# A two-block transformer kernel: attention of a group placed among the projections of the next, heads in row and column pairs, memory keys and values made in the first block

## The chip, the cores and the metric

The kernel runs on one core of one Trainium2 chip. The metric is the device time in microseconds (us) of one execution. Engines are named as the profile names them: PE is TensorE (matrix products; PEld its weight loads), DVE is VectorE, ACT is ScalarE, POOL is GpSimd, SP issues most DMAs. All data is f32; "fp32r" is a one-pass f32 format of PE.

## The reference, cut to what matters

The program is two blocks in sequence. The first is a dilated-window attention over three groups of eight heads and a convolutional feed-forward; the second a layer with three attentions (differential, windowed, and over a memory of 256 tokens), gates, and sixteen experts. The sequence is 512 tokens of width 1024.

```python
# first block: three groups, windows 128/512/2048, dilations 1/4/16, 8 heads of 64
proj = (h @ w_in).reshape(B, S, 3, 3, 8, 64)            # per group: q, k, v
for g, (window, dilation) in enumerate(ATTN_GROUPS):
    q = rms_norm(proj[:, :, g, 0], q_gain[g]) * scale
    k = rms_norm(proj[:, :, g, 1], k_gain[g])
    o, lse = dilated_window_attention(q, k, proj[:, :, g, 2], window, dilation)
weights = softmax(stack(lses), axis=0)
x = x + sum(weights * outs) @ w_out
x = x + conv_ffn(rms_norm(x, ffn_norm), ...)
# second block
h, m = rmsnorm(x, attn_norm_g), rmsnorm(mem, mem_norm_g)
o_da = rmsnorm(diff_attention(...), subln_g) * 0.8      # 8 heads of 128
o_wa = window_attention(...)                            # 16 heads of 64
mk, mv = split(m @ w_mem_kv, 2)                         # mem is an input: no dependence on x
o_xa = memory_attention(xa_q, mk, mv)                   # 4 heads of 256
x = x + (g0 * (o_da @ w_da_o) + g1 * (o_wa @ w_wa_o) + g2 * (o_xa @ w_xa_o)) @ w_out
x = x + expert_choice_ffn(rmsnorm(x, ffn_norm_g), ...)
return rmsnorm(x, final_norm_g)
```

## The kernel before

Everything is written by hand for each engine, with semaphores; the order of the code of an engine is the order in which it runs. A dense product is made in three fp32r passes: the weights are split into a high and a low part (`w_hi`, `w_lo`), the activations too, and high x high, high x low and low x high are summed. SP loads weights in chunks of 1 MB into a ring of four slots. POOL splits each chunk in two **halves**: it writes the high part (L457), then the low part (L460); ACT writes the high part of the halves in `by_act` (L775) and POOL only the low one. There are two buffers, so half i may be split once PE has used half i-2. One half feeds 24 PE products of 512 columns.

**First block.** PE takes the three groups one after the other. For each it makes eight blocks of queries and keys in `to_features` (L1332 to L1334), each followed by the mean square of the block before (L1405, a product with `mean64`), and four halves of values in `to_tokens` (L1348 to L1350). ACT squares (L620) and takes the root (L626), DVE takes the reciprocal (L920) and scales (L932). Then the attention of the group runs in **units** of four blocks of 128 x 128: scores (L1426 in group 0, L1429 after it) of one head against keys that are padded with zeros to 128 rows (`k1_odd` for the odd heads), mask and row maximum on DVE (L943, L946), exponentials on ACT (L636), four transposes on PE (L1455), the copy of these on DVE (L954), and the product with the values (L1444, L1447), whose result ACT copies (L648). There are 16, 8 and 8 units. Within a unit each step waits for the one before, and PE has the scores, transposes and value products of neighbouring units to fill in, nothing else.

After the last group comes the **combination**: PE transposes the row statistics (L1461), DVE copies them (L965) and works out a coefficient for each head, group and token (L967 to L980, with ACT's L650), PE spreads each over 64 rows (L1468), DVE multiplies and adds (L987, L990), ACT and DVE split the sum (L654, L995, L998), and the output product follows in `out_proj`.

**Second block.** The windowed attention (scores L1588, transposes L1595, value products L1617) runs in 16 units plus a tail, with the projection of `xa_q` spread over the slots by the table `FILL2` (`proj_part`, L1530 to L1532). POOL makes a mask scale for each pair of heads and splits one half between (L509, `split(stage["f2"] + p + 1)`). Then comes the **memory stage**: the norm of the memory tokens, their transposes (L1376), eight blocks of keys (24 products of 256 columns each, L1380 and L1332 to L1334), with a mean square of one differential head after each block, and four blocks of values (L1348 to L1350); DVE scales the differential heads there (L1143, L1145). Then the **memory attention** (scores L1657, transposes L1677, values L1667), and the gates. The experts' 16 x 24 chunks of 1 MB end the program.

## Time and profile before

| | us |
|---|---|
| median of 3 runs (lowest, highest) | 2649.49 (2647.84, 2649.54) |
| the profiled execution | 2650.34 |
| its span, first to last instruction | 2648.6 |
| PE / DVE / ACT / POOL busy in it | 2362.2 / 929.0 / 502.4 / 1026.7 |
| granted TensorE clock, mean | 0.973 |

The table of stretches in the rows below gives the busy time of each engine in one stage. A busy PE is not PE at its peak, and a group's busy share does not say whether it lies on the path: for that, read which stage has nothing else to do on PE. Times in the rows count from the start of the span.

### The profile page before, as it was taken

To read this page: it belongs to the slowest core of one execution; us is meant where nothing else is said; L and a number is where in the kernel's file an instruction comes from. 1 tells how busy PE (TensorE), PEld (TensorE's weight loads), DVE (VectorE), ACT (ScalarE), POOL (GpSimd) and SP (SyncE) were. 2 spreads that over 40 slices of the span, in tenths; PEclk is the share of its full clock that TensorE was granted. 3 is DMA by queue.
4 is the path that set the end of the run, shared out by engine and by line. 5 is a ranking of instruction groups with operands and counts; after the bars stand their busy time and mean duration, and the time that the engine had idled before them with its cause. 6 is when DMAs were issued, how large, how long until landed. Compare 5 with 4: busy or idle time off the path is not lost.

```text
span 2648.6 us, 27075 instructions
## 1 busy us (share of the span) xinstructions
PE 2362.2 (89%) x11257; PEld 1558.1 (59%) x11257; DVE 929.0 (35%) x1313; ACT 502.4 (19%) x1076; POOL 1026.7 (39%) x499
## 2 busy tenths in 40 slices
PE   6999968999998998898899999799988888888886
PEld 4777837888787866576678888433323233332322
DVE  5654674555102047665622264211110101111012
ACT  2324232112002034476321010100000000000001
POOL 5444605888778754453548887100000000000000
PEclk9999979999999999998999999799999999999999
DMA  4111201233222321111312225699999999999996
GB/s 145 65 48 48 80 16 48 96 96 98 102 101 69 102 72 32 37 44 33 127 48 96 96 96 221 243 417 417 418 418 418 417 417 416 416 418 417 418 417 282
DMA packets 172341, 527.43 MB, mean 199 GB/s; under 512 B 9954, under 2 KB 92091, under 8 KB 139451
## 3 DMA queue, kind: packets, MB, share of 16 engines
q1 hardware_dynamic: 169008, 521.17, 50.7%
q10 hardware_dynamic: 3211, 4.51, 0.5%
q8 instruction: 90, 1.47, 0.3%
q14 instruction: 32, 0.26, 0.0%
HBM read 523.56 MB, written 2.10 MB: 198 GB/s over the span
## 4 chain that ended last, share of the span: by engine, by line
PE 73%; DMA 13%; DVE 9%; ACT 2%; issue 2%; ACTq 0%; POOL 0%; SPq 0%; DVEq 0%; POOLq 0%
DMA arena<-in_w_exp_up 9%; PE ps L1332 9%; PE ps L1334 9%; PE ps L1333 9%; PE ps L1834 8%; PE ps L1807 7%; PE ps L1495 5%; DMA ring<-in_w_exp_up 4%; PE ps L1348 3%; PE ps L1349 3%; PE ps L1350 3%; PE ps L1765 2%; PE ps L1789 1%; PE ps L1551 1%; PE ps L1530 1%
## 5 line engine op out<-in xcount | busy, mean ns | idle before, releaser
L457 POOL TENSOR_TENSOR w_hi<-ring,one 128x1024 fp32r<-128x1024 f32 x208 | 406.2, 1953 | 504.8 <-PE ps L1334 243.9
L460 POOL TENSOR_TENSOR w_lo<-ring,w_hi 128x1024 fp32r<-128x1024 f32 x222 | 542.7, 2445 | 57.3 <-ACT w_hi L775 41.1
L1332 PE MATMUL ps<-h_hi,w_hi 128*128 128x512 f32 x840 | 335.1, 399 | 2.6 <-ACT arena L648 1.8
L1334 PE MATMUL ps<-h_hi,w_lo 128*128 128x512 f32 x840 | 327.2, 389 | 0.0
L1333 PE MATMUL ps<-h_lo,w_hi 128*128 128x512 f32 x840 | 327.0, 389 | 0.0
L555 POOL TENSOR_TENSOR arena<-arena 128x512 f32<-128x512 f32 x8 | 8.4, 1049 | 810.8 <-PE ps L1777 794.0
L1807 PE MATMUL ps<-arena 128*64 128x512 f32 x944 | 213.0, 595 | 42.8 <-DMA arena<-in_w_exp_up 42.8
L1807 PE MATMUL ps<-ring,arena 128*64 128x512 f32 x944 | 213.1, 595 | 41.7 <-DMA ring<-in_w_exp_up 40.1
L1332 PEld LDWEIGHTS ps<-h_hi,w_hi 128*128 128x128 f32 x840 | 157.7, 188 | 42.7 <-issue 5.6
L1333 PEld LDWEIGHTS ps<-h_lo,w_hi 128*128 128x128 f32 x840 | 157.7, 188 | 35.8 <-issue 4.3
L1807 PEld LDWEIGHTS ps<-arena 128*64 128x64 f32 x944 | 71.5, 137 | 180.9 <-issue 180.6
L1334 PEld LDWEIGHTS ps<-h_hi,w_lo 128*128 128x128 f32 x840 | 157.7, 188 | 33.3
L1807 PEld LDWEIGHTS ps<-ring,arena 128*64 128x64 f32 x944 | 71.1, 137 | 179.0 <-issue 176.8
L1268 DVE TENSOR_TENSOR arena<-ps,arena 64x1024 f32<-64x1024 f32 x32 | 39.3, 1227 | 287.6 <-ACT arena L853 286.9
L853 ACT ACTIVATE arena<-ps 64x1024 f32<-64x1024 f32 x32 | 30.8, 1010 | 568.1 <-PE ps L1807 568.1
L1277 DVE TENSOR_TENSOR x<-ps,x 128x512 f32<-128x512 f32 x64 | 42.9, 689 | 260.9 <-PE ps L1789 260.4
L920 DVE RECIPROCAL arena<-arena 128x512 f32<-128x512 f32 x24 | 80.5, 3353 | 63.1 <-ACT arena L626 63.0
L1834 PE MATMUL ps<-arena 128*64 128x512 f32 x432 | 95.7, 593 | 5.5 <-DVE arena L1299 5.5
L1021 DVE SCALAR_TENSOR_TENSOR arena<-ps,vec,arena 128x511 f32<-128x511 f32 (+1 forms) x88 | 59.9, 743 | 114.2 <-ACT arena L665 114.2
L1834 PE MATMUL ps<-ring,arena 128*64 128x512 f32 x416 | 92.2, 593 | 5.5 <-DVE arena L1299 5.5
L1306 DVE COPY arena<-ps 64x512 f32<-64x512 f32 x16 | 11.1, 694 | 223.8 <-PE ps L1834 223.8
L863 ACT ACTIVATE arena<-ps 64x512 f32<-64x512 f32 x16 | 9.5, 591 | 349.3 <-PE ps L1834 349.3
(324 smaller groups left out, 3916.6 us busy)
## 6 DMA issues: line engine op xcount, KB each, us to landing
ring<-in_w_exp_gate SPq DMA_DIRECT2D x59, 1024.0 KB, 24.1
ring<-in_w_exp_up SPq DMA_DIRECT2D x59, 1024.0 KB, 25.4
arena<-in_w_exp_gate SPq DMA_DIRECT2D x59, 1024.0 KB, 23.8
arena<-in_w_exp_up SPq DMA_DIRECT2D x59, 1024.0 KB, 25.5
arena<-in_w_exp_down SPq DMA_DIRECT2D x54, 1024.0 KB, 20.1
ring<-in_w_exp_down SPq DMA_DIRECT2D x52, 1024.0 KB, 22.0
ring<-in_w_in SPq DMA_DIRECT2D x34, 1024.0 KB, 5.2
ring<-in_ffn_w_up SPq DMA_DIRECT2D x22, 1024.0 KB, 5.0
```

What stands on the lines that cost most here:

```text
L457: nc.gpsimd.tensor_tensor(hi, w, one[:].unsqueeze(2).to_broadcast(list(w.shape)), ALU.mult).then_inc(w_high, 1)
L460: nc.gpsimd.tensor_tensor(lo, w, hi.bitcast(f32), ALU.subtract).then_inc(w_split, 1)
L920: V.reciprocal(rr[:, n % 2, :], rt[:, n % 2, :]).then_inc(rr_done, 1)
L1332: mm(o, w[0][:, k, :], h[0][:, k, 0:ntok], start=(k == 0), stop=False)
L1333: mm(o, w[0][:, k, :], h[1][:, k, 0:ntok], start=False, stop=False)
L1334: last = mm(o, w[1][:, k, :], h[0][:, k, 0:ntok], start=False, stop=(k == KT - 1))
L1348: mm(o, hi, w[0][:, k - k0, :], start=(k == 0), stop=False)
L1349: mm(o, hi, w[1][:, k - k0, :], start=False, stop=False)
L1350: last = mm(o, lo, w[0][:, k - k0, :], start=False, stop=(k == nk - 1))
L1495: last = mm(ps[:, 2 * t + half, :], tile_of(a_, f, t), w_[:, 0, half * 512:half * 512 + 512], start=(f == 0 and a_ is act_hi and w_ is w[0 ...
L1807: last = mm(ps[64 * i:64 * i + 64, c, :], xeT[:, k, a * CAP:(a + 1) * CAP], w[:, c * 512:c * 512 + 512], start=(k == 0), stop=(k == KT - 1))
L1834: last = mm(ps[64 * half:64 * half + 64, 4, :], act_e[:, f, :], w[:, j * D + half * 512:j * D + half * 512 + 512], start=(f == 0), stop=(f ...
```

## The change

1. **Order of work in the first block.** A group's values are now made first, then its queries and keys. The projections of group g+1 are cut into 24 pieces of 12 products (`v_part`, `qk_part`). Four of them, or six pieces of memory keys for the last group, run before the attention of group g, the others in its slots (`fills`, `FILL`). In the slots of the last group stand the memory's keys (`mk_part`), in the combination the memory's values (`mv_part`). `qk` and `v1` are doubled.
2. **Pairs.** A unit is now two heads over one or two query tiles. The scores of the two heads use rows 0 to 63 and 64 to 127 of PE, with no zero padding; in group 0 one product spans 256 keys. The value products of the two heads write rows 0 to 63 and 64 to 127 of one bank.
3. **Who does what.** ACT, not DVE, copies the transposes. DVE copies the raw block out of its bank (`raw`) and scales it later (`scaled`). Square, root and exponential now alternate on ACT. The projections use banks 4 to 7, the attention 0 to 3.
4. **Memory.** Its norm runs among group 0's projections. Keys and values go to DRAM during the feed-forward and come back before the windowed attention. ACT writes the high part of six halves, not of fourteen.
5. **Combination.** Four banks in turn; the row copies no longer wait for each other; the output product starts after all multiplications are done and two of the four parts are split.
6. **Second block.** The memory stage is gone. The mean squares of the differential heads are summed in one bank in slots 12 to 15 of the windowed attention (`da_sum`), whose projection of `xa_q` now takes 12 slots of 3, 3 and 2 steps in turn, not 16 of 4. One root and one reciprocal of 8 x 512 follow; eight products spread the result over the rows during the memory attention, where DVE scales the eight heads. Scores of the memory attention use two banks, not four.

```diff
-NORM_TILES = [TT, TT, TT, MEM // P, TT]
+NORM_TILES = [TT, MEM // P, TT, TT, TT]
...
-        for j in range(8):
-            FILL2[2 * j] = ((j, range(2)), (j, range(2, 4)))
-            FILL2[2 * j + 1] = ((j, range(4, 6)), (j, range(6, 8)))
+        third = (range(3), range(3, 6), range(6, 8))
+        for u in range(12):
+            FILL2[u] = tuple((i // 3, third[i % 3]) for i in (2 * u, 2 * u + 1))
...
+            split_rows(tok_chunks(w1, b + 2 * GW, GW), v_ps, TT * (g + 1))
             split_cols(col_chunks(w1, b, 2 * GW), qk_ps, 8 * g)
-            split_rows(tok_chunks(w1, b + 2 * GW, GW), v_ps, TT * (g + 1))
+        split_cols(col_chunks(wm, 0, D), mk_ps, 0)
+        stage["mem_v"] = len(halves)
+        for half in range(2):
+            split_rows(tok_chunks(wm, D + 512 * half, 512), mk_ps, 8 + 2 * (half + 1))
+        by_act = range(stage["mem_v"] + 2, len(halves))
...
+            for p in range(HEADS1 // 2):
+                units += [(g, p, [t]) for t in range(TT)] if g == 0 else [(g, p, [0, 1]), (g, p, [2, 3])]
...
+        def fills(g):
+            if g + 1 < GROUPS:
+                todo = [("v", 2 * m + i, part) for m in range(2) for part in range(2) for i in range(2)]
+                todo += [("qk", 8 * (g + 1) + b, half) for b in range(8) for half in range(2)]
+            else:
+                todo = [("mk", j, half) for j in range(8) for half in range(2)]
+            first, n = (4, 4, 6)[g], UB[g + 1] - UB[g] + 2
+            rest = todo[first:]
+            return [todo[:first]] + [rest[u * len(rest) // n:(u + 1) * len(rest) // n] for u in range(n)]
...
-                split(stage["f2"] + p + 1)
+                split(stage["f2"] + min(p + 2, 8))
...
+                for i in range(L + 4):
...
+                    for n in ended(g, i, "qk"):
+                        square(n)
...
+                    for n in ended(g, i - 1, "qk"):
+                        root(n)
...
+                        act.wait_ge(nm_done, u + 1)
...
+                    if 1 <= i <= L:
+                        act.wait_ge(t_ps, m + 1)
                         if m >= 2:
...
+                            act.wait_ge(pv_done, m - 1)
+                        A(pt1[:, m % 2, :], ps[:, 2, :], F.Copy).then_inc(pt_done, 1)
...
+            def scaled(n):
...
+                dve.wait_ge(rt_done, n + 1)
+                V.reciprocal(rt[:, n % 4, :], rt[:, n % 4, :]).then_inc(rr_done, 1)
+                dve.wait_ge(rr_done, n + 1)
+                dve.wait_ge(qr_done, n + 1)
+                V.scalar_tensor_tensor(out=o, in0=o, scalar=vec[:, gain:gain + 1], in1=r, op0=ALU.mult,
+                                       op1=ALU.mult).then_inc(qk_done, 1)
...
+                for i, f in enumerate(FILL[g][0]):
+                    fill(g, f)
+                    if i == 1:
+                        for n in [7] if g == 0 else ended(g - 1, UB[g] - UB[g - 1] + 2, "qk"):
+                            mean_sq(n)
...
+                    for f in todo[0:1]:
+                        fill(g, f)
+                    m = u - 1
+                    if 1 <= i <= L:
+                        pe.wait_ge(p_done, m + 1)
+                        if m:
+                            pe.wait_ge(pt_done, m)
+                        for j in range(4):
+                            last = nc.tensor.transpose(ps[:, 2, j * P:(j + 1) * P], sm[:, m % 3, j * P:(j + 1) * P], ident[:])
+                        last.then_inc(t_ps, 1)
+                    for f in todo[1:2]:
+                        fill(g, f)
+                    for n in ended(g, i, "qk"):
+                        mean_sq(n)
...
+            mv_part(1, 0)
+            mv_part(1, 1)
             pe.wait_ge(coef_done, 1)
...
+            def last_oT(i):
+                pe.wait_ge(oT_low, 4)
+                pe.wait_ge(mk_ev, 12)
+            pe.wait_ge(oT_low, 2)
+            pe.wait_ge(bc_done, 12)
             out_proj((oT_hi, oT_lo), 4, wo_ps)
...
+                def da_sum(h):
+                    pe.wait_ge(pjA, PJ[:J_M].count("A"))
+                    pe.wait_ge(on_sq, h + 1)
+                    mm(ps[0:DA_H, 3, :], head_col[:, 7 - h:15 - h], osq[:, h % 2, :], start=(h == 0), stop=(h == 7)).then_inc(on_ps, 1)
+                if 12 <= u < 16:
+                    da_sum(2 * (u - 12))
...
+            dve.wait_ge(on_rt, 1)
+            V.reciprocal(ort, ort).then_inc(on_rr, 1)
...
+                        mm(ps[:, 6 + h % 2, :], ident[0:DA_H, h:h + 1].to_broadcast([DA_H, P]), ort, start=True, stop=True).then_inc(on_ps, 1)
```

**PE in the attention of group 0.** Before, one unit after the other; `ps` is PSUM, `arena` the working memory, `ident` the identity:

```order
L1455 MATMUL ps<-ident,arena 128x128 [waits pt_done,p_done]
L1455 MATMUL ps<-ident,arena 128x128 x3
L1426 MATMUL ps<-arena 128x128 [waits sm_done]
L1426 MATMUL ps<-arena 128x128 x3
L1444 MATMUL ps<-arena 64x128 [waits pt_done]
L1444 MATMUL ps<-arena 64x128 x3
```

And after, one slot of group 0, in which half a block of group 1's queries stands (12 products, of which the first three and the last are shown):

```order
L1612 MATMUL ps<-arena 128x256 [waits sm_done]
L1612 MATMUL ps<-arena 128x256
L1490 MATMUL ps<-h_hi,w_hi 128x512 [waits w_split,qr_done,sq_done]
L1491 MATMUL ps<-h_lo,w_hi 128x512
L1492 MATMUL ps<-h_hi,w_lo 128x512
...
L1492 MATMUL ps<-h_hi,w_lo 128x512
L1623 MATMUL ps<-ident,arena 128x128 [waits pt_done,p_done]
L1623 MATMUL ps<-ident,arena 128x128 x3
L1504 MATMUL ps<-arena,mean 128x512 [waits sq_done,rt_done]
L1640 MATMUL ps<-arena 64x128 [waits pt_done]
L1640 MATMUL ps<-arena 64x128 x3
```

The scores are two products of 256 columns where four of 128 stood, and a piece of the projection and now and then a mean square stand between a unit's steps.

**ACT in the attention of group 0.** Before, two units (L636 the exponentials, L648 the copy of a head's result):

```order
L636 ACTIVATE arena,l<-arena,nm 128x256 [waits nm_done]
L636 ACTIVATE arena,l<-arena,nm 128x256
L636 ACTIVATE arena,l<-arena,nm 128x256 [waits nm_done]
L636 ACTIVATE arena,l<-arena,nm 128x256
L648 ACTIVATE arena<-ps 64x512 [waits pv_done]
```

And after, two slots (L652 square, L659 root, L700 exponentials, L708 the copy of the transposes):

```order
L652 ACTIVATE arena<-ps 128x512 [waits ssq_ps,qk_ps]
L700 ACTIVATE arena,l<-arena,nm 128x256 [waits nm_done]
L700 ACTIVATE arena,l<-arena,nm 128x256
L708 ACTIVATE arena<-ps 128x512 [waits pv_done,t_ps]
L659 ACT_TABLE_LOAD [waits qk_done]
L659 ACTIVATE arena<-ps,epsb 128x512 [waits ssq_ps]
L700 ACT_TABLE_LOAD
L700 ACTIVATE arena,l<-arena,nm 128x256 [waits nm_done]
L700 ACTIVATE arena,l<-arena,nm 128x256
L708 ACTIVATE arena<-ps 128x512 [waits pv_done,t_ps]
```

A table load stands now before a root and before the exponentials that follow it; the whole program has 36 table loads where it had 18.

**PE after the windowed attention.** Before, its last value products are followed by the memory stage (transposes of the memory tokens, keys):

```order
L1617 MATMUL ps<-arena 64x128 x9
L1376 MATMUL ps<-ident,arena 128x128 [waits pjD,n_xn,pjA,w_split,wpt_done,wO_ev]
L1376 MATMUL ps<-ident,arena 128x128 x7
L1376 MATMUL ps<-ident,arena 128x128 [waits n_evD]
L1376 MATMUL ps<-ident,arena 128x128
L1380 MATMUL ps<-mem_hi,w_hi 128x256
```

And after, by the scores of the memory attention and, from L1885 on, the products that spread a differential head's factor:

```order
L1845 MATMUL ps<-arena 64x128 x9
L1876 MATMUL ps<-arena 128x256 [waits pjD,sw_done,pjA,in_mem,wpt_done,wO_ev]
L1876 MATMUL ps<-arena 128x256 x7
L1876 MATMUL ps<-arena 128x256 [waits xe1_done]
L1876 MATMUL ps<-arena 128x256 x3
L1876 MATMUL ps<-arena 128x256 [waits xe1_done]
L1876 MATMUL ps<-arena 128x256 x3
L1885 MATMUL ps<-arena,ident 128x512 [waits on_rr] x2
```

The whole memory stage has left this place; a wait for `on_rr`, the one reciprocal, has come.

## Rows read from the trace of the kernel before

**Rows 1.** Stretches: us, busy us of PE, PEld, DVE, ACT, POOL; PEclk, DMA, GB/s.
```profile
22.90:106.50 83.60, 81.13 (x340) 64.36 (x340) 45.66 (x33) 17.30 (x28) 50.27 (x28) 1.00 0.23 77
106.50:151.60 45.10, 40.41 (x321) 35.28 (x321) 33.05 (x48) 23.95 (x74) 4.25 (x2) 1.00 0.08 25
151.60:225.90 74.30, 73.55 (x304) 61.63 (x305) 40.54 (x20) 14.06 (x22) 47.87 (x23) 1.00 0.22 71
225.90:252.50 26.60, 21.32 (x163) 18.25 (x164) 16.48 (x24) 22.22 (x73) 3.58 (x2) 1.00 0.13 41
252.50:328.10 75.60, 74.82 (x319) 62.87 (x317) 41.36 (x22) 15.25 (x22) 49.86 (x24) 1.00 0.22 70
328.10:353.50 25.40, 20.15 (x144) 17.07 (x144) 16.99 (x24) 21.18 (x72) 1.61 (x1) 0.93 0.14 43
353.50:394.40 40.90, 17.60 (x48) 6.96 (x48) 33.59 (x44) 4.00 (x5) 0.00 (x0) 0.73 0.00 0
1122.90:1238.30 115.40, 110.96 (x801) 80.94 (x800) 70.79 (x240) 76.03 (x229) 49.40 (x28) 0.97 0.16 52
1238.30:1310.90 72.60, 59.79 (x320) 48.70 (x321) 49.06 (x40) 31.11 (x43) 37.42 (x16) 0.90 0.30 99
1310.90:1346.00 35.10, 31.85 (x128) 21.41 (x128) 16.54 (x43) 13.39 (x40) 4.90 (x3) 1.00 0.11 36
```

**Rows 2.** Timeline of PE, group 0: a block of queries begins, a mean square.
```profile
39.24 0.39 PE L1332 MATMUL ps<-h_hi,w_hi 128*128 128x512 f32 x1
...
44.68 1.02 PE L1405 MATMUL ps<-arena,mean 128*128 128x512 f32 x2
```

**Rows 3.** Timeline of PE, one unit of group 0 (start, us, what).
```profile
118.45 0.66 PE L1455 MATMUL ps<-ident,arena 128*128 128x128 f32 x4
118.94 1.06 PE L1426 MATMUL ps<-arena 128*128 128x128 f32 x8
119.93 1.09 PE L1444 MATMUL ps<-arena 128*64 128x128 f32 x8
120.95 0.66 PE L1455 MATMUL ps<-ident,arena 128*128 128x128 f32 x4
```

**Rows 4.** Timeline of PE, windowed attention: pairs of heads, full and half clock.
```profile
1160.87 1.35 PE L1588 MATMUL ps<-arena 64*128 64x256 f32 x8
...
1163.90 1.31 PE L1617 MATMUL ps<-arena 128*64 128x128 f32 x20
...
1235.85 2.40 PE L1617 MATMUL ps<-arena 128*64 128x128 f32 x20 [0.47 <-ACT arena L731]
```

**Rows 5.** Timeline of ACT: root after square, its table load between.
```profile
11.06 0.19 ACT L595 ACTIVATION_READ_ACCUMULATOR arena<-x 128x1 f32 x1
11.27 1.28 ACT L597 ACT_TABLE_LOAD   x1
12.56 0.29 ACT L597 ACTIVATE ssq<-ssq,epsb 128x1 f32<-128x1 f32 x1
```

**Rows 6.** Costliest groups of the page: POOL's two steps, DVE's reciprocal.
```profile
L457 POOL TENSOR_TENSOR w_hi<-ring,one 128x1024 fp32r<-128x1024 f32 x208 | 406.2, 1953 | 504.8 <-PE ps L1334 243.9
L460 POOL TENSOR_TENSOR w_lo<-ring,w_hi 128x1024 fp32r<-128x1024 f32 x222 | 542.7, 2445 | 57.3 <-ACT w_hi L775 41.1
L920 DVE RECIPROCAL arena<-arena 128x512 f32<-128x512 f32 x24 | 80.5, 3353 | 63.1 <-ACT arena L626 63.0
```

**Rows 7.** Timeline, combination: coefficients wait, last product, output product.
```profile
373.47 7.47 PE L1468 MATMUL ps<-arena 128*128 128x512 f32 x10 [17.18 <-DVE arena L980]
...
391.50 0.69 DVE L987 TENSOR_TENSOR arena<-ps,arena 128x512 f32<-128x512 f32 x1
...
394.41 0.80 PE L1348 MATMUL ps<-w_hi,oT_hi 128*128 128x512 f32 x1 [3.22 <-DVE oT_lo L998]
```

**Rows 8.** Timeline of PE, memory stage: two products of 256 columns in a row.
```profile
1247.65 0.28 PE L1381 MATMUL ps<-mem_lo,w_hi 128*128 128x256 f32 x1
...
1247.77 0.28 PE L1382 MATMUL ps<-mem_hi,w_lo 128*128 128x256 f32 x1
```

684 lines of the change are left out of this document (399 added, 285 removed).

## The prediction, made before the changed kernel was run

> **What bounds the kernel now.** I read the stretches first. From 22.9 us on PE is almost never idle while it makes projections: 81.1 of 83.6 us in group 0, 73.6 of 74.3 in group 1, 74.8 of 75.6 in group 2 [rows 1]. Between them lie three attentions (45.1, 26.6 and 25.4 us) in which PE is busy 40.4, 21.3 and 20.2 us, with products that before this change use half of its rows or columns. Then come two stretches in which PE is poorly used: the combination, 40.9 us with DVE busy 33.6, PE 17.6 and a granted clock of 0.73, and the memory stage, 72.6 us with PE busy 59.8 and POOL 37.4. The memory stage depends on nothing in the first block. So the change stands or falls with two questions: how much PE time the pairs free in the first block, and whether the memory's work fits there.
>
> Next the units. In group 0 one cycle takes 2.50 us of PE time: transposes 0.49, scores 0.99, value products 1.02 [rows 3]. The nearest rows for pairs are those of the windowed attention: four score products with 1280 columns in 1.35 us, ten value products of 128 columns in 1.31 us, about 0.13 each against 0.26 in group 0 [rows 3, 4]. Two heads on opposite halves of PE do run at once here. At the end of that stage the same ten value products take 2.40 us: that is the lower of the two clock levels, 1.2 instead of 2.4 GHz, after PE had waited several times [rows 4].
>
> **The sum, stage by stage.** Prices: a piece of 12 products is 2.72 us (24 from 39.24 to 44.68 take 5.44), a mean square about 0.9 of the 1.02 shown [rows 2]. A unit will cost scores 0.5 (two of 256 columns at once) in 12 of group 0's units and 0.8 elsewhere, since the eight weight loads remain, transposes 0.5, value products 0.5: 25 us for group 0, 14.4 for each other group. Bounds: 0.5 if the 128-column pairs overlap fully, 0.99 and 1.02 if not at all [rows 3]. I add 0.3 us per slot for waits when PE changes from one kind of work to the next; no row shows such a slot. The nearest is PE's wait of 0.47 for a copy [rows 4], so 0 to 0.6.
>
> *Group 0's projections* (83.6 us): the same twelve halves, values first; the memory's norm adds 16 short transposes, and two large memsets leave DVE. No change, -2 to +4.
>
> *Attention 0 with group 1's projections* (45.1 + 74.3 = 119.4 us). Before the first slot: four pieces 10.9, two mean squares 1.8, and a wait of about 0.9 for POOL, whose two steps take 1.95 + 2.45 = 4.4 us per half [rows 6], while the second half's buffer is free only when the last block is done. In that time the last block's chain (root 0.7, reciprocal 3.35, scaling 1.0) ends as well. Slots: 20 pieces 54.4, seven mean squares 6.3, units 25, 18 x 0.3 = 5.4, and 1.9 for POOL at the third and fourth half of the values, whose buffers come free one piece apart. Sum 13.6 + 93.0 = **106.6**, that is -12.8.
>
> *Attention 1 with group 2's projections* (26.6 + 75.6 = 102.2 us). 13.6 before the slots, 54.4 + 6.3 + 14.4 + 10 x 0.3, 1.1 for the strided activations, 2.7 for POOL, since two pieces now stand in a slot: **95.5**, -6.7. DVE needs 6.4 us per slot here (copy 0.7, mask and maximum 1.4, reciprocal 3.35, scaling 1.0) against 8.5 of PE; still covered.
>
> *Attention 2 with the memory's keys* (25.4 us). A key product of 256 columns takes 0.12 us [rows 8], a piece 1.44, a half 2.9, less than POOL's 4.4. Six pieces before the slots take about 12 us, bound by POOL and by the last block's chain alike. Ten slots: ten pieces 14.4, units 14.4, gaps 3, and some 1.2 for the first unit. Then 1.4 for the last copy: **46.4**, +21.0. So the three attentions together change by only +1.5: what the pairs free is spent on the keys.
>
> *Combination* (40.9 us, and the output product behind it). The values need eight pieces, 21.8 us of PE, where PE waited 17.18 us for the coefficients [rows 7] and on in between. They hide. The path is DVE's: it loses little by the unlinked copies (0.3) and by four banks and a warm clock at the first products (2.5), may wait 1 us for a piece that PE has begun, and the output product starts at the end of the multiplications instead of 2.9 us later (391.50 + 0.69 against 394.41 less the handover, [rows 7]). -3.7 in all. Its first twelve products ran at half clock, 0.43 instead of 0.23 us, and should not now: -2.5. Together **-6.2**.
>
> *Windowed attention* (115.4 us, PE busy 111.0: PE bounds it). Eight products of 512 columns for the sums of squares, at 0.9, add 7.2; the fill is only repacked. In slots 12 to 15 ACT gets two squares (0.6 each) and may set the pace by a little. POOL has to split a half every 1.5 slots of 7.7 us, 4.4 + 2.6 for the scales: enough. **+8**, bounds +7 and +12.
>
> *Memory stage*: **-72.6**, all of it, its POOL and DMA work too. The 2 MB written and read back lie beside the feed-forward and the windowed attention.
>
> *Memory attention* (35.1 us, PE busy 31.9). Eight spreading products at 0.9 add 7.2. One reciprocal of 3.35 and a root with a table load (1.3 + 0.7) stand before the first row maximum on DVE, so the first exponentials start about 5.4 us after the windowed attention ends, not 1.6; PE has only the first scores meanwhile and starts at the lower clock. I take 5 us for that. **+12**, bounds +7 and +16.
>
> Sum: -12.8 - 6.7 + 21.0 - 6.2 + 8 - 72.6 + 12 = **-57.3**. From 2650.34 that gives 2593.0; the execution profiled lies 0.85 above the median, so 2592.
>
> **A rule against this change.** ACT now changes its function table twice around a root, in eleven places. In the trace a root starts as soon as its table load is over: the step before ends at 11.25, the load runs from 11.27 for 1.28 us, the root starts at 12.56 [rows 5]. Two slots of group 0 then need 7.6 us of ACT against 9.9 of PE; a slot of group 1 needs 6.4 against 8.5. The Trainium skill, page "ScalarE: Activation LUTs", section "What ACT_TABLE_LOAD costs", puts a switch at 2.66 us, since the engine also drains for 1.38 us. This case's rows show no such drain; by the page ACT would need more time than PE in those slots.
>
> **The rivals.**
>
> *ACT sets the pace* (chance 0.17). If each of 22 loads took twice its 1.28 us, ACT would need 10.2 in two slots of group 0 and 9.0 in one of group 1, over PE's 9.9 and 8.5: +4 us at least, and 28 if all of it lay on the path, since root, exponentials and the copy of the transposes stand in one queue and PE waits for each of them. In the middle 2608. For it: exponentials and roots were never mixed before. Against it: rows 5. The page's figure above is this case.
>
> *Pairs of 128 columns do not overlap* (0.06). Scores back to 0.99, value products to 1.02: 6 + 3 + 17 = 26 us, 2618. Against it: rows 4. This is also the case in which the change does not do what it says.
>
> *Tighter than I think* (0.18). No gaps (-11), nothing lost at the start of the memory attention (-5): 2576.
>
> *Slower than before* (0.03). In the last group's slots and the combination PE has little work between waits. If PE got the lower clock there and in the slots before, every us of PE work would cost another. The gain is used up once 57 us of work run at 1.2 GHz; with all of attention 2's 35 us and 35 of the combination at half clock and some of group 1's it would be 2665. For it: the clock was 0.93 in attention 2 and 0.73 in the combination [rows 1]. Against it: these slots will be fuller than before.
>
> *No change* (0.01): half of the above.
>
> **How the numbers follow.** The forecast, 2592 within 2580 to 2604, has 0.55. The range 2570 to 2620 takes in the tight case and most of the two that cost; outside lie the slow case and the worst of the ACT case. About 0.2% (5 us) is what can be told from no change. Faster 0.96, same 0.01, slower 0.03.
>
> **What would show it.** In the changed profile: the attention-with-projection stretches at 107, 96 and 46 us with PE busy over 0.9 of them; the value products L1640 at 0.5 us for eight records; ACT's loads at 1.28 with the next ACTIVATE right behind; waits for POOL's L460 of some us before each first slot; the combination at 37 us with PE busy over 0.8; no stretch between L1845 and L1876; DVE's 8 x 512 reciprocal followed by the first maximum. I would be wrong if the gaps per slot were over 0.6 us, if attention 2 took over 55 us because keys wait for POOL, or if the memory attention took over 52.

## The result, and the profile after

The changed kernel takes 2623.44 us (median of four runs, 2622.06 to 2623.97); the kernel before took 2649.51 beside it. The ratio is 0.9902, with a 95% interval of 0.9885 to 0.9919: 26 us faster, where I had forecast 57. The profiled execution of the changed kernel has a span of 2620.3 us, 28.3 less than before's 2648.6.

The stretches of the changed kernel, cut where those of [rows 1] were cut. The columns are start and end, length, busy us of PE, PEld, DVE, ACT and POOL, the granted clock, the share of the DMA engines and GB/s:

```profile
22.90:106.30 83.40, 80.02 (x353) 64.84 (x354) 41.40 (x43) 21.23 (x40) 48.98 (x27) 0.98 0.24 77
106.30:215.30 109.00, 105.06 (x562) 79.77 (x560) 66.33 (x57) 54.56 (x115) 53.75 (x25) 1.00 0.18 58
215.30:309.80 94.50, 91.64 (x467) 73.02 (x465) 61.04 (x40) 45.90 (x106) 54.99 (x25) 0.98 0.21 67
309.80:357.80 48.00, 42.79 (x356) 37.28 (x354) 24.66 (x22) 27.20 (x89) 36.65 (x17) 0.93 0.26 88
357.80:411.80 54.00, 39.42 (x145) 26.00 (x145) 44.54 (x42) 11.54 (x15) 26.69 (x12) 0.91 0.29 97
411.80:436.40 24.60, 23.86 (x96) 19.25 (x96) 7.45 (x12) 4.57 (x8) 13.48 (x7) 0.92 0.14 44
1139.30:1268.60 129.30, 116.81 (x817) 80.80 (x816) 69.81 (x240) 78.03 (x234) 49.46 (x28) 1.00 0.16 54
1268.60:1317.90 49.30, 43.73 (x145) 25.64 (x145) 24.32 (x45) 15.61 (x43) 0.00 (x0) 0.93 0.00 0
```

In the order of the sum, in us:

| stage | before | forecast | after | after less forecast |
|---|---|---|---|---|
| group 0's projections | 83.6 | 83.6 | 83.4 | -0.2 |
| attention 0 with group 1's projections | 119.4 | 106.6 | 109.0 | +2.4 |
| attention 1 with group 2's | 102.2 | 95.5 | 94.5 | -1.0 |
| attention 2 with the memory's keys | 25.4 | 46.4 | 48.0 | +1.6 |
| combination | 40.9 | 37.2 | 54.0 | +16.8 |
| output product | 25.3 | 22.8 | 24.6 | +1.8 |
| windowed attention | 115.4 | 123.4 | 129.3 | +5.9 |
| memory stage | 72.6 | 0 | 0 | 0 |
| memory attention | 35.1 | 47.1 | 49.3 | +2.2 |

The last column adds up to 29.5; the span missed the forecast by 29.0 us (28.3 gained, not 57.3). More than half of it is one row, the combination. It was to become shorter and grew by 13.1.

Here are DVE's chain for the coefficients in the combination of the changed kernel, and POOL beside it (timelines: start, us, engine, line, operation, what it writes and reads, idle time before it and who ended that):

```profile
365.01 1.76 DVE L1046 TENSOR_TENSOR arena<-arena 8x512 f32<-8x512 f32 x1
366.81 0.68 DVE L1047 TENSOR_TENSOR arena<-arena 8x512 f32<-8x512 f32 x1
367.52 4.06 DVE L1049 TENSOR_TENSOR arena<-arena 8x512 f32<-8x512 f32 x3
373.13 4.03 DVE L1053 TENSOR_TENSOR arena<-arena 8x512 f32<-8x512 f32 x3 [1.55 <-ACT arena L727]
377.20 2.76 DVE L1055 TENSOR_TENSOR arena<-arena 8x512 f32<-8x512 f32 x1
380.00 0.68 DVE L1056 TENSOR_TENSOR arena<-arena 8x512 f32<-8x512 f32 x1
380.71 3.34 DVE L1057 RECIPROCAL arena<-arena 8x512 f32<-8x512 f32 x1
384.09 4.41 DVE L1059 TENSOR_TENSOR arena<-arena 8x512 f32<-8x512 f32 x3
```

```profile
363.83 2.40 POOL L483 TENSOR_TENSOR w_lo<-ring,w_hi 128x1024 fp32r<-128x1024 f32 x1 [3.44 <-ACT w_hi L639]
367.46 2.38 POOL L483 TENSOR_TENSOR w_lo<-ring,w_hi 128x1024 fp32r<-128x1024 f32 x1 [1.23 <-ACT w_hi L639]
374.21 5.21 POOL L483 TENSOR_TENSOR w_lo<-ring,w_hi 128x1024 fp32r<-128x1024 f32 x2 [4.38 <-ACT w_hi L639]
382.23 2.39 POOL L483 TENSOR_TENSOR w_lo<-ring,w_hi 128x1024 fp32r<-128x1024 f32 x1 [2.81 <-ACT w_hi L639]
385.33 2.63 POOL L483 TENSOR_TENSOR w_lo<-ring,w_hi 128x1024 fp32r<-128x1024 f32 x1 [0.72 <-ACT w_hi L639]
```

Read the two together. L1047 and L1056 run while POOL stands still and take 0.68 us. The same kind of operation at L1055 starts at 377.20, in the middle of POOL's two steps that last until 379.42, and ends at 379.96, 0.54 us after POOL was through. L1046, L1049 and L1053 each have one such stop; L1059's three meet the end of one step and the whole of the next. The reciprocal, with one input, takes 3.34 as before. In the kernel before, POOL was idle in this stage ([rows 1], 0.00 busy). The same chain there, from the row statistics on PE to the last three products on DVE:

```profile
353.51 1.47 PE L1461 MATMUL ps<-ident,nm 128*8 128x128 f32 x12 [1.15 <-ACT arena L648]
...
366.74 0.68 DVE L976 TENSOR_TENSOR arena<-arena 8x512 f32<-8x512 f32 x1
...
371.54 1.88 DVE L980 TENSOR_TENSOR arena<-arena 8x512 f32<-8x512 f32 x3
```

The first coefficient product came 20.0 us after the row statistics (353.51 to 373.47, [rows 7]), and now comes 30.7 us after them (357.84 to 388.56):

```profile
388.56 5.31 PE L1660 MATMUL ps<-arena 128*128 128x512 f32 x8 [4.52 <-DVE arena L1059]
```

### The profile page after: what moved, and what is told of

Same layout as the page of the kernel before. It is cut to its first block, busy times and chain, and to the rows that moved or that the text cites. A ratio compares the mean times of both kernels' runs of the same rounds, so it can differ in the third digit from the quotient of the medians.

```text
span 2620.3 us, 26993 instructions
## 1 busy us (share of the span) xinstructions
PE 2349.5 (90%) x11209; PEld 1528.1 (58%) x11209; DVE 902.4 (34%) x1264; ACT 518.4 (20%) x1111; POOL 1046.5 (40%) x508
## 4 chain that ended last, share of the span: by engine, by line
PE 72%; DMA 14%; DVE 9%; issue 2%; ACT 1%; POOL 1%; ACTq 0%; SPq 0%; DVEq 0%; POOLq 0%
DMA arena<-in_w_exp_up 9%; PE ps L2062 9%; PE ps L1402 7%; PE ps L1404 7%; PE ps L1403 7%; PE ps L2035 7%; PE ps L1714 5%; DMA ring<-in_w_exp_up 4%; PE ps L1993 2%; PE ps L1418 2%; PE ps L1419 2%; PE ps L1420 2%; PE ps L1490 2%; PE ps L1492 1%; PE ps L1491 1%
## 5 line engine op out<-in xcount | busy, mean ns | idle before, releaser
L480 POOL TENSOR_TENSOR w_hi<-ring,one 128x1024 fp32r<-128x1024 f32 x216 | 421.9, 1953 | 481.7 <-PE ps L1404 179.3
L483 POOL TENSOR_TENSOR w_lo<-ring,w_hi 128x1024 fp32r<-128x1024 f32 x222 | 548.8, 2472 | 29.5 <-ACT w_hi L639 12.6
L1404 PE MATMUL ps<-h_hi,w_lo 128*128 128x512 f32 x656 | 255.5, 389 | 0.0
L1403 PE MATMUL ps<-h_lo,w_hi 128*128 128x512 f32 x656 | 255.4, 389 | 0.0
L1402 PEld LDWEIGHTS ps<-h_hi,w_hi 128*128 128x128 f32 x656 | 123.2, 188 | 29.3 <-DVE arena L1234 1.6
L1404 PEld LDWEIGHTS ps<-h_hi,w_lo 128*128 128x128 f32 x656 | 123.2, 188 | 25.7
L1403 PEld LDWEIGHTS ps<-h_lo,w_hi 128*128 128x128 f32 x656 | 123.2, 188 | 25.1
L993 DVE RECIPROCAL arena<-arena 128x512 f32<-128x512 f32 x24 | 80.3, 3346 | 16.8 <-ACT arena L659 16.7
## 6 DMA issues: line engine op xcount, KB each, us to landing
ring<-in_w_exp_up SPq DMA_DIRECT2D x59, 1024.0 KB, 25.4
arena<-in_w_exp_up SPq DMA_DIRECT2D x59, 1024.0 KB, 25.4
```

The source lines that it names most:

```text
L480: nc.gpsimd.tensor_tensor(hi, w, one[:].unsqueeze(2).to_broadcast(list(w.shape)), ALU.mult).then_inc(w_high, 1)
L483: nc.gpsimd.tensor_tensor(lo, w, hi.bitcast(f32), ALU.subtract).then_inc(w_split, 1)
L993: V.reciprocal(rt[:, n % 4, :], rt[:, n % 4, :]).then_inc(rr_done, 1)
L1402: mm(o, w[0][:, k, :], h[0][:, k, 0:ntok], start=(k == 0), stop=False)
L1403: mm(o, w[0][:, k, :], h[1][:, k, 0:ntok], start=False, stop=False)
L1404: last = mm(o, w[1][:, k, :], h[0][:, k, 0:ntok], start=False, stop=(k == KT - 1))
```

## The experiments

Times are medians; each kernel differs from the changed kernel only by the edit shown, unless it says otherwise. The kernel before, run beside them, took 2648.61 to 2650.36, so a difference of 1 or 2 us between two kernels is not told from none.

**e1 and e2: what makes the combination long.**

In e1 it is POOL's `split`:

```diff
+                    if i in by_act:
+                        w, hi, lo = (v[:, :, 0:2] for v in (w, hi, lo))
                     nc.gpsimd.tensor_tensor(lo, w, hi.bitcast(f32), ALU.subtract).then_inc(w_split, 1)
```

In e2, PE's `mv_part`:

```diff
-                        mm(o, tile_of(mem_hi, kb, t), w[0][:, k, :], start=(kb == 0), stop=False)
-                        mm(o, tile_of(mem_hi, kb, t), w[1][:, k, :], start=False, stop=False)
-                        last = mm(o, tile_of(mem_lo, kb, t), w[0][:, k, :], start=False, stop=(kb == KT - 1))
+                        if k == 0:
+                            last = mm(o, tile_of(mem_hi, kb, t), w[0][:, k, :], start=(i == 0), stop=(i == 3))
```

> The low parts of six halves of the memory's value weights, which POOL makes between 363.8 and 388 us beside DVE's chain for the coefficients, are cut to two columns of each block of 128 or 512, so the values computed are not exact; everything else, the high parts, the waits and all products on PE, stays. Theory A (DVE's additions, subtractions and products whose two inputs both lie in SBUF stand still while POOL works): the chain from the first transposed row statistic (L1653) to the first coefficient product (L1660) falls from 30.7 us to 20 to 22, L1049's three from 4.1 to about 1.9 us, L1059's three from 4.4 to 1.9; the kernel gets 9 to 12 us faster than the changed one, about 2613 us. Theory B (the value pieces that PE does in front of the coefficient products delay them): chain and time as in the changed kernel, 2622 to 2624, at most 2 us less since fewer pieces wait for POOL.

> Of the 96 products for the memory's values in the combination only 16 are made (one of six per weight half and token tile), so the values are wrong; POOL and ACT split all weight halves as before. Theory A (DVE stands still while POOL works): the six low parts still fall into DVE's chain, only closer together; the first coefficient product comes 27 to 31 us after the first row statistic, the kernel gains at most 4 us over the changed one (the pieces between the coefficient products gone). Theory B (PE's pieces are in the way): the chain is back at about 20 us, the kernel 10 us or more faster than the changed one.

e1 took 2611.51 us, 11.9 less than the changed kernel. DVE's chain in e1:

```profile
364.30 0.68 DVE L1048 TENSOR_TENSOR arena<-arena 8x512 f32<-8x512 f32 x1
...
365.73 1.89 DVE L1051 TENSOR_TENSOR arena<-arena 8x512 f32<-8x512 f32 x3
...
371.09 0.68 DVE L1057 TENSOR_TENSOR arena<-arena 8x512 f32<-8x512 f32 x1
```

All are back at 0.68 or 1.9 for three; the coefficients come after 20.7 us (357.13 to 377.82). e2 took 2617.25, 6.2 less: with hardly any value pieces on PE the chain still lasts 27.7 us, and DVE still stops beside POOL:

```profile
364.44 2.72 DVE L1047 TENSOR_TENSOR arena<-arena 8x512 f32<-8x512 f32 x1
...
377.44 2.73 DVE L1056 TENSOR_TENSOR arena<-arena 8x512 f32<-8x512 f32 x1
```

So theory A holds for the chain: POOL's steps beside it cost 10 us. Of the 3.0 us by which e2's chain is shorter, 1.4 are the six row copies, the last two of which stand behind a piece in the changed kernel (6.43 us, in e2 5.06); the other 1.6 are stops, since POOL's steps, closer together, add 8.4 us to DVE's operations and not 10.0. The output product starts 3.8 us earlier in all (407.95), within the 4 that I had allowed; the medians differ by 2 us more than that, the profiled spans by 4.2.

**e3 and e5: do the pairs run side by side?**

In e3 the scores, and likewise the value products:

```diff
+                        for h in range(2):
                             for j, t in enumerate(tiles):
                                 for s_ in range(2) if (g, t) == (0, 0) else (0,):
-                                    for h in range(2):
```

In e5 this on top:

```diff
-                                    r = slice(64 * h, 64 * h + 64)
+                                    r = slice(0, 64)
-                                    last = mm(ps[64 * h:64 * h + 64, 3, t * P:(t + 1) * P],
+                                    last = mm(ps[0:64, 3, t * P:(t + 1) * P],
```

> Same products as in the changed kernel, but in every unit of the first block first all scores and value products of one head, then those of the other, so two neighbours seldom lie on opposite halves of PE. If neighbours on opposite halves run at once (my price for the pairs), a unit's value products go from 0.66 us for eight records to about 1.1, its scores from 0.72 to about 1.0, and with 32 units the kernel loses 15 to 25 us against the changed one (2638 to 2648). If the pairs bring nothing beyond the single order, no more than 2 us.

> Both heads of every unit of the first block are computed on the same half of PE: scores of both read rows 0 to 63, value products of both write output rows 0 to 63 (so the second head's part is wrong and half of the attention's output is left as it was); counts, columns and waits are those of the run with the heads apart, in which nothing changed (8 value products 0.66 us, time 2623.4). Theory A (products on opposite halves of PE overlap even when they are four apart): now they can't, eight value products take about 1.1 us as in the kernel before, scores 1.0, and the kernel loses 15 to 25 us, to 2638 to 2648. Theory B (nothing overlaps; a product of 128 columns simply costs 0.06 us here, and the kernel before paid for something else): 0.66 us as now and 2622 to 2625.

e3 took 2623.40 us: no change at all, against my 15 to 25. Had I stopped there, I would have concluded that the pairs bring nothing. e5 took 2647.22, 23.8 more. One unit's value products (L1640) and scores (L1612) in group 0, in the order changed kernel, e3, e5:

```profile
187.23 0.66 PE L1640 MATMUL ps<-arena 128*64 128x128 f32 x8
187.82 0.70 PE L1612 MATMUL ps<-arena 64*128 64x256 f32 x4
```

```profile
187.09 0.66 PE L1640 MATMUL ps<-arena 128*64 128x128 f32 x8
187.69 0.70 PE L1612 MATMUL ps<-arena 64*128 64x256 f32 x4
```

```profile
196.24 1.09 PE L1640 MATMUL ps<-arena 128*64 128x128 f32 x8
197.26 1.13 PE L1612 MATMUL ps<-arena 64*128 64x256 f32 x4
```

The profile has two records for each of these products. On one half of PE the four products (eight records) take 1.09, exactly what [rows 3] show for the kernel before. On two halves they take 0.66, whether the halves alternate or come two products by two. So the overlap is real, worth 24 us in all, and does not need the two products to be neighbours. From one start to the next the value products take 0.59 us (187.23 to 187.82), near my 0.5, and the rival "pairs of 128 columns do not overlap" is refuted.

**e6: the same combination without DVE's long operations.** The coefficients are computed with the tokens on the partitions (`nms`, the negated maxima, and `tk` are 128 partitions x 32 elements per group, `crow` and `rows` were 8 x 512) and transposed afterwards, between the first and the second value piece; `p_` is the PSUM bank of the coefficient product.

```diff
-            link(V.tensor_tensor(crow[:, 0, :], rows[:, 0, :], rows[:, 1, :], ALU.min))
+            link(V.tensor_tensor(tk[:, 0, :], nms[:, 0, :], nms[:, 1, :], ALU.min))
...
-                    link(V.tensor_tensor(oT[:, b, :], oT[:, b, :], ctmp[:, n % 2, :], ALU.add))
+                    link(V.tensor_tensor(p_, p_, U[:, g, b, :], ALU.mult))
+                    V.tensor_tensor(oT[:, b, :], p_, oT[:, b, :], ALU.add).then_inc(bc_done, 1)
...
             mv_part(0, 0)
+            pe.wait_ge(c_tok, 1)
...
+            mv_part(0, 1)
+            coefs(0, 1, 2, 3)
+            mv_part(0, 2)
+            coefs(4, 5)
...
```

> All is computed. The coefficients are made with the tokens on the partitions, 32 or 96 elements wide instead of 8 rows of 512, and only then transposed; group 0's maxima and sums are brought into the strided order of tokens before group 2's units; the sums over the groups are formed in PSUM, so that each DVE addition has one input there; the value pieces of the memory stand between the coefficient products. Theory A (DVE's long chain and its standing still beside POOL cost the 13 us by which the combination grew, and 4 more that I had expected to gain): the first coefficient product comes 8 to 10 us after the last copy of group 2 instead of 31, the combination takes 30 to 36 us instead of 54, now bound by PE and POOL, and the kernel comes to 2600 to 2606. If POOL's splitting itself, 3.5 us a half for eight halves and then 4.6 us for each of the output weights, sets the combination's length, it stays at 45 us or more and the kernel at about 2614.

It took 2604.10 us, 19.3 less than the changed kernel. The stretch from the last copy of group 2 to the output product, then PE and DVE in it:

```profile
355.20:394.50 39.30, 34.09 (x132) 23.38 (x133) 25.59 (x35) 12.59 (x17) 23.18 (x11) 1.00 0.33 107
```

```profile
361.03 1.48 PE L1690 MATMUL ps<-ident,arena 128*8 128x128 f32 x12 [1.61 <-DVE arena L1067]
...
365.12 3.59 PE L1682 MATMUL ps<-arena 128*128 128x512 f32 x8
...
394.52 0.47 PE L1431 MATMUL ps<-w_hi,oT_hi 128*128 128x512 f32 x1 [2.41 <-POOL w_lo L485]
```

```profile
356.88 2.35 DVE L1061 TENSOR_TENSOR arena<-arena,nm 128x96 f32<-128x96 f32 x1
359.58 0.26 DVE L1063 TENSOR_TENSOR arena<-arena,l 128x96 f32<-128x96 f32 x1 [0.35 <-ACT arena L736]
```

The stretch is 39.3 us long, 3 over my upper end; in the changed kernel the same stretch lasted 55.2 (356.61 to 411.78). The coefficients come 10 us after the copy, and now PE and POOL set the pace: the output product waits for POOL's halves. Several edits stand together in e6 (the chain, the additions, the order of the pieces), so its 19.3 us are not divided among them. L1061 shows that an operation need not be large to be stopped: 96 elements per partition, the size that L1063 does in 0.26 us, take 2.35, until a step of POOL that runs from 356.65 for 2.47 us is over.

**e12: only the additions read one input from PSUM.**

```diff
-                    link(V.tensor_tensor(oT[:, b, :], oT[:, b, :], ctmp[:, n % 2, :], ALU.add))
+                    link(V.tensor_tensor(p_, p_, U[:, g, b, :], ALU.mult))
+                    V.tensor_tensor(oT[:, b, :], p_, oT[:, b, :], ALU.add).then_inc(bc_done, 1)
```

> All is computed. Against the changed kernel only the combination's last part differs: a product coefficient times output stays in its PSUM bank, and the addition reads it from there, so it has one input in SBUF instead of two. The chain for the coefficients, with its two-SBUF operations, is as it was. In the changed kernel four of the eight additions (L1069) took 0.9 to 2.0 us instead of 0.69 while POOL worked, 4.2 us in all. If it is the second SBUF input that makes DVE stand still, all eight additions take 0.7 us and the output product starts 2 to 4 us earlier, 2619 to 2621.5. If any DVE operation on 128 x 512 elements is slowed by POOL, or the pieces of PE between the coefficient products set the pace there, less than 1 us changes.

All eight additions take 0.69 us now, also beside POOL:

```profile
402.27 0.69 DVE L1070 TENSOR_TENSOR arena<-ps,arena 128x512 f32<-128x512 f32 x1
407.82 2.41 DVE L1076 TENSOR_TENSOR oT_lo<-arena,oT_hi 128x512 fp32r<-128x512 f32 x1
```

The rule for the additions held (401.23 to 403.61 and 407.33 to 409.68 are steps of POOL), yet the kernel took 2624.64, no less, where I had expected 2619 to 2621.5. From the first coefficient product to the output product it is 23.6 us as against 23.2: DVE waits 2.16 us for PE's pieces there, and the low part L1076, which still has both inputs in SBUF, takes the stop instead. PE also waited longer ahead of the first coefficient products (4.91 us, not 4.52), and the first eight took 6.08 us, not 5.31, longer at the lower clock level; that is 0.8 us against the edit. Removing a stop pays only where DVE is last.

**e4, e7, e9, e13, e14: the windowed attention, 14 us longer instead of 8.**

e4, with ACT's squares cut likewise:

```diff
+                    n = 2 if h else S
-                    mm(ps[0:DA_H, 3, :], head_col[:, 7 - h:15 - h], osq[:, h % 2, :], start=(h == 0), stop=(h == 7)).then_inc(on_ps, 1)
+                    mm(ps[0:DA_H, 3, 0:n], head_col[:, 7 - h:15 - h], osq[:, h % 2, 0:n], start=(h == 0), stop=(h == 7)).then_inc(on_ps, 1)
```

e7, where `pieces` are the 24 pieces in their order, of 3, 2, 3 and 2, 3, 3 blocks, and the squares stand in ACT's slots 13 to 16, behind the exponentials:

```diff
-        for u in range(12):
-            FILL2[u] = tuple((i // 3, third[i % 3]) for i in (2 * u, 2 * u + 1))
+        for u in range(14):
+            FILL2[u] = (pieces.pop(0), pieces.pop(0) if u < 10 else ())
-                if 12 <= u < 16:
-                    da_sum(2 * (u - 12))
+                if 14 <= u < 18:
+                    da_sum(2 * (u - 14))
```

e9 has these pieces in twelve slots and the sums where they were; its squares stand in ACT's slots 11 to 14, behind the exponentials:

```diff
-                if 12 <= u < 16:
-                    for h in (2 * (u - 12), 2 * (u - 12) + 1):
+                if 11 <= u < 15:
+                    for h in (2 * (u - 11), 2 * (u - 11) + 1):
```

e13 and e14, the former with the cut of e4 as well; the squares stand in ACT's slots 15 to 17:

```diff
+        for j in range(8):
+            FILL2[2 * j] = ((j, range(2)), (j, range(2, 4)))
+            FILL2[2 * j + 1] = ((j, range(4, 6)), (j, range(6, 8)))
+                if u >= 16:
+                    da_sum(4 * (u - 16))
```

> In the windowed attention seven of the eight squares on ACT and of the eight products for the sums of squares on PE are cut from 512 columns to 2, so the differential attention's norm is not exact. The stage took 129.9 us against 115.4 before the change; I had forecast +8. If the sums alone cost what is missing, the stage falls to about 116 us and the kernel gains 13. If the sums cost their 7 us of products and some 4 of waits (1.08 us in each of the last four slots for a square on ACT), and the rest is that the projections now stand in twelve slots in which PE waits 0.96 us in every third for ACT's copy L819, the stage is 119 to 120 us, the kernel gains 9 to 11.

> All is computed. In the windowed attention the 24 pieces of the projections are spread over fourteen slots instead of twelve, never with fewer than two blocks before the value products except in odd jobs' first piece; the eight sums of squares stand in the last four slots, where PE waits for the chain anyway, and their squares are made one slot earlier, behind the exponentials. The stage took 129.4 us, 14 more than before; I count 7.2 for the sums' products and 7 for PE's waits in slots without projections. If that reading is right, the stage falls to 121 to 124 us and the kernel to 2616 to 2619. If the sums only take the place of waits, as in the run with the sums cut (2 us less for the stage), and the waits follow the last slots wherever they stand, the stage stays at 127 or more.

> All is computed. In the windowed attention the projections stay in twelve slots, but no slot has fewer than three blocks ahead of the value products except once in three jobs, and the squares for the sums are made one slot earlier, behind the exponentials. It tells the two kinds of wait apart from the place of the sums, which stay in slots 12 to 15. In the changed kernel PE waits 0.96 us in every third of the twelve slots (3.8 in all) and 1.08 us for a square in each of the last four (4.3). If these waits are what the stage lost beyond the sums' own products, it falls from 129.4 to 121 to 123 us, the kernel to 2615 to 2618. If the chain scores, maximum, exponential, scaling, transposes, copy sets the length of a slot that has no projections, only the first part goes: 125 to 127 us, 2619 to 2622.

> The projections stand in sixteen slots of the windowed attention, as before the change; the eight sums stand in the last two slots and seven of them, with their squares, are cut to two columns, so the differential attention's norm is not exact. From the first scores of the windowed attention to the first of the memory attention the changed kernel took 129.3 us. Theory A (the four emptied slots and the uneven pieces cost 7 us, the sums 7): the stage is 115 to 117 us. Theory B (the stage grew for another reason, say the transfers of the kept keys and values beside it or waits at its start): it stays over 119.

> All is computed. As in the run beside it, but with the sums whole: eight products of 512 columns and their squares in the last two slots, where PE waited for about 5 us before the change. Theory A: the stage takes 119 to 122 us, 7 to 10 less than in the changed kernel, since part of the sums lies in waits; the root and its reciprocal then start after the last sum, so the memory attention keeps its 49 us; 2614 to 2617 if the clock of the stages behind stays, up to 4 us more if the router's products run at the lower level as in e4 and e7. Theory B: 125 us or more.

PE in the changed kernel, one of three such slots with projections and one of the four without:

```profile
1171.36 1.31 PE L1845 MATMUL ps<-arena 128*64 128x128 f32 x20 [0.96 <-ACT arena L819]
...
1250.74 1.02 PE L1827 MATMUL ps<-arena,head_col 128*8 128x512 f32 x2 [1.08 <-ACT arena L832]
```

The stage, from its first scores to the first of the memory attention:

| | stage, us | kernel, us |
|---|---|---|
| changed kernel | 129.3 | 2623.44 |
| e4, sums cut | 127.2 | 2627.90 |
| e7, fourteen slots, sums in the last four | 125.1 | 2622.09 |
| e9, twelve slots, squares earlier | 127.0 | 2626.05 |
| e13, sixteen slots, sums cut | 115.3 | 2610.51 |
| e14, sixteen slots, sums in the last two | 120.7 | 2618.05 |

e4's stage missed its expectation by 7 us, e9's is that of its second theory (125 to 127), e7's lies 1 over its range. When the sums or ACT's delay went, the next link of the unit's chain (DVE's scaling, ACT's copy) ended last in the four slots that have no projections; a slot fell from 7.0 only to 5.5 to 5.7 in e4 and 6.4 to 6.6 in e9. e13 and e14 bring the old length back:

```profile
1142.30:1257.60 115.30, 111.49 (x817) 79.93 (x816) 68.41 (x240) 75.68 (x234) 49.04 (x28) 1.00 0.18 60
```

```profile
1140.60:1261.30 120.70, 116.90 (x817) 80.24 (x816) 68.39 (x240) 79.93 (x234) 49.03 (x28) 1.00 0.17 58
```

With the projections in all sixteen slots and the sums cut, the stage has its old length, 115.3. The sums add 5.4 (e14). The other 8.6 are the twelve slots together with the place of the sums: e14 also has them in the last two slots, where PE had waits before, and no run has sixteen slots with the sums in slots 12 to 15. In e7, with the sums in the last four slots and the projections in fourteen, 4.2 of the 8.6 are gone. PE's work is the same in e14 and in the changed kernel (116.9 and 116.8 busy); what differs is 8.6 us of waiting.

The kernels' times don't follow the stages exactly. In the profiled executions e4 and e7 give back 3.7 us in the router's products, which ran at the lower of the two clock levels for longer; e7's was one of its two slower executions (2624.10 and 2623.62; the others 2620.55 and 2619.85). The router's products in the changed kernel and in e4 (ns min/median/max, first and last start):

```profile
L1946 PE MATMUL ps<-wr,hT x64: 177/263/376, 1625.3 to 1635.8; 128*128 128x16 f32 x64
```

```profile
L1948 PE MATMUL ps<-wr,hT x64: 177/374/393, 1624.2 to 1638.4; 128*128 128x16 f32 x64
```

e9 gives its gain back at once: the memory attention behind it takes 53.9 us instead of 49.3, with more of its products at half clock (granted clock 0.84, not 0.93). e14's profiled execution is its fastest, 2613.31 us, and the other three took 2617.74 to 2618.56, so the worth of its 8.6 us in the whole kernel, 5 us by the medians, is known only roughly.

**e10: the root before the memory attention.**

```diff
-            act.wait_ge(on_ps, 8)
-            A(ort, ps[0:DA_H, 3, :], F.Sqrt, bias=epsb[0:DA_H]).then_inc(on_rt, 1)
...
+                if u == 16:
+                    act.wait_ge(on_ps, 8)
+                    A(ort, ps[0:DA_H, 3, :], F.Sqrt, bias=epsb[0:DA_H]).then_inc(on_rt, 1)
```

> All is computed. ACT makes the root for the differential attention's norm in slot 16 of the windowed attention instead of after its end, so DVE's reciprocal of 3.34 us, which stands ahead of the memory attention's first maxima, can run before the memory attention begins. If root, two table loads and reciprocal are what delays the memory attention's first exponentials (my forecast: 5.4 us instead of 1.6 after the start), PE's first transposes there come 3 to 4 us earlier and the kernel gains 3 to 4 us, 2619 to 2620.5. If the table loads in the tail delay ACT's copies there by as much (PE waits for L819 there already), nothing is gained.

2620.32 us, 3.1 less, as expected. DVE in the changed kernel and in e10:

```profile
1270.59 3.34 DVE L1215 RECIPROCAL arena<-arena 8x512 f32<-8x512 f32 x1 [8.24 <-ACT arena L854]
1273.86 1.21 DVE L1220 TENSOR_REDUCE nmx<-ps 128x2 f32<-128x512 f32 x2
```

```profile
1266.11 3.34 DVE L1216 RECIPROCAL arena<-arena 8x512 f32<-8x512 f32 x1 [2.73 <-ACT arena L830]
1271.68 0.69 DVE L1221 TENSOR_REDUCE nmx<-ps 128x2 f32<-128x512 f32 x1 [2.23 <-PE ps L1877]
```

The memory attention shrinks from 49.3 to 46.1 us (1269.65 to 1315.78).

**e8, e11, e15, e16: the edits together.** e8 is e6 with e7, e11 is e6 with e9 and e10, e15 is e6 with e14, e16 is e6 with e10.

> All is computed: coefficients by token and the windowed attention's sums later, together. The two edits lie 750 us apart and share nothing, so their gains should add: 17 to 23 us and 4 to 7 us, 2594 to 2602 us. If the clock granted in the stages behind changes with the shorter stages, as the time behind the memory attention did in the run with the sums cut (3 us), up to 4 us more or less.

> All is computed: coefficients by token (2604.1 alone), squares earlier with the even packing, and the root in the tail. If the gains add: 19.3 and what the two runs beside this one give, 5 to 8 and 3 to 4 us together, 2593 to 2597. In the run with the coefficients and the sums later the second gain was lost (2603.4), so if the memory attention takes up whatever the stage ahead gives, it stays at 2601 or more.

> All is computed: coefficients by token (2604.1 alone) and the sixteen slots with the sums behind. If the gains add, 2594 to 2598.

> All is computed: coefficients by token and the root in slot 16, the windowed attention as in the changed kernel. Its gains alone were 19.3 and 3.1; if they add, 2601. The run with the earlier squares as well had 2597.3 although those alone had lost 2.6; 2597 or less here would say that the squares bring nothing in that company either.

e8 took 2603.44 us (0.7 less than e6), e11 2597.28, e15 2598.59, e16 2601.32. e16 is what the two gains add up to. e11 is 4.0 below e16, although its one further edit (e9) had lost 2.6 alone: its windowed attention is 127.0 us long, as in e9, but its memory attention takes 44.5 us, where e16's takes 46.1 and e9's 53.9. Taken each against the kernel before beside it, e11 and e16 are 51.3 and 48.3 us faster, and the intervals of the two ratios overlap (0.9796 to 0.9825, 0.9801 to 0.9834). e8 missed its 2594 to 2602: e7's gain was small alone, and the router's products ran slow as above (14.2 us). e15 missed the 2594 to 2598 by 0.6. The lowest median is e11's: ratio to the kernel before 0.9810, interval 0.9796 to 0.9825, 26 us below the changed kernel; e15 cannot be told from it.

## Why the prediction was wrong, point by point

**What held.** The three attentions were to change by +1.5 us together and changed by +4.5. The unit's price, the 0.3 us of gaps per slot and PE's waits for POOL ahead of the first slots were about right: PE waited for L483 six times, 5.8 us in all, and for L996 2.9 us, in the whole stretch from 106 to 357. The memory stage's 72.6 us went to nothing, as said. That the pairs run at once is what e5 showed; it is worth 24 us.

**ACT does not set the pace.** A root in a slot of group 0 in the changed kernel:

```profile
165.86 0.60 ACT L652 ACTIVATE arena<-ps 128x512 f32<-128x512 f32 x1 [1.09 <-PE ps L1492]
166.47 1.28 ACT L659 ACT_TABLE_LOAD   x1
167.77 0.69 ACT L659 ACTIVATE arena<-ps,epsb 128x512 f32<-128x512 f32 x1
168.48 1.28 ACT L700 ACT_TABLE_LOAD   x1
```

The load begins 0.01 us after the square has ended and takes 1.28 us, as in [rows 5]; the root follows at once. By the rule of the Trainium skill weighed in the prediction (page "ScalarE: Activation LUTs", section "What ACT_TABLE_LOAD costs") 1.38 us of draining should stand there. The trace disagrees, and PE waits for ACT only once in these stretches, 0.3 us ahead of a transpose (L1623, for the copy L708).

**The step that failed: "They hide. The path is DVE's: it loses little by the unlinked copies".** I had asked what PE's eight pieces do to the path and found that they fit into PE's waits. I had not asked what the pieces bring with them: POOL must split eight halves of weights, in the one stage in which POOL was idle before and in which DVE is last. My sum had -3.7 for the combination; it measured +13.1. Of these 16.8 us, 10 are DVE's stops in the chain (e1: 30.7 to 20.7 us). One more is the row copies, which took 6.43 us, 5.71 before, where I had taken 0.3 off.

The other 5.8 lie between the first coefficient product and the output product: 23.2 us, 20.9 before, where my sum allowed 17.5. Of these, 1.6 are gone in e1, where PE's wait is shorter and the first eight coefficient products take 3.70 us instead of 5.31; the warm clock that I had counted on for them did not come in the changed kernel. With six of POOL's steps gone e1's stage is 42.3 us (357.13 to 399.42), still 5 over the forecast, 4.1 of it in this part. Pieces on PE and stops in the additions both stand there, and neither e2 (22.4 us with few pieces) nor e12 (23.6 without the stops) shortens it by much. How they share the 4.1 is open.

The term was also added up wrongly: 0.3, 2.5 and 2.9 less 1 are 4.7, not 3.7, and [rows 7] leave at most 2.2 for the start of the output product (392.19 to 394.41), not 2.9. That step itself came true: the last multiplication ends at 411.68 and the output product starts at 411.78.

My own [rows 7] showed L987 at 0.69 us, but with POOL at zero beside it ([rows 1]); a duration carries over to a new place only if its neighbours do.

The stop is a rule of the Trainium skill, page "SBUF — State Buffer", section "🔬 SBUF: two separate sides": the ports that DVE and GpSimd share are held by whichever instruction starts first until it ends, if DVE's has two inputs in SBUF, and the other "fully blocks". e1 (0.68 us again), e6's L1061 (2.35 us) and e12's additions (0.69 us beside POOL) agree with it. It speaks against this change, and the prediction did not weigh it.

**The scaling in the attentions was priced too low.** I had 1.0 us. L996 reads its two inputs from SBUF now, where before one came from PSUM, and takes 1.8 in the mean from 106.7 to 357.8 us, with POOL at work; the two ahead of group 2's first scores took 3.14 and 1.73, and PE waits 2.7 us for the second. That this is the same stop is not shown, as no run changes this operation alone:

```profile
L996 DVE SCALAR_TENSOR_TENSOR arena<-arena,vec 128x512 f32<-128x512 f32 x18 | 32.3, 1795 | 0.6
```

**The output product.** -2.5 for the end of the half clock was too much. The combination's clock did rise, from 0.73 [rows 1] to 0.91, but PE's last wait in it is 5.56 us, and the first nine products behind that wait still start 0.43 us apart, where it had been the first twelve. The stage gained 0.7.

**"The fill is only repacked".** The windowed attention's +7.2 for the sums was near (5.4, e14 against e13), but the packing into twelve slots was no neutral edit: it left four slots in which PE has only the unit's own chain and the sums. With the place of the sums this cost 8.6 us (e14 against the changed kernel). The words "may set the pace by a little" for ACT there were the right place with the wrong size.

**Memory attention.** +12 forecast, +14.2 measured; root and reciprocal were the reason named, and moving them gave 3.1 (e10).

**The range.** Its upper end, 2620, took in the ACT case but no case in which the combination grows. I set no bounds for that stage, and the only loss in its sum was 1 us for a piece on PE, although POOL, which was idle there before, was to work in it.

## What to carry to other kernels

When work is moved under a wait of one engine, list what every other engine must do for it, and ask which of their operations meet those of the engine that is last there. In these runs a DVE operation with both inputs in SBUF that started during a step of POOL ended only after it (2.76 us for 0.68), and one with an input in PSUM did not stop (0.69, e12); keep one input in PSUM, or make the operations so few and short that most fall between POOL's steps, as in e6. And work that fills the gaps of a chain is not free to move: emptying four slots of it and putting the sums there cost 8.6 us more than the sums do (5.4) when all sixteen slots keep it.

## What the runs showed that I had not expected

Products on opposite halves of PE overlap even when two of one half come first and two of the other after them (e3: 0.66 us for the four, alternating or not; on one half 1.09 us, e5). A shorter stage can cost time later: in e4 and e9 the stage became 2 us shorter and the kernel 4.5 and 2.6 us longer, in e7 4 us shorter and the kernel only 1.4 shorter; in their profiles products behind it ran longer at the lower clock level. What decides that is open. It is not simply how long PE waited in the stage itself: that was 12.5 us in the changed kernel, 14.6 in e4, 8.9 in e7 and 9.1 in e9.
